# First attention of a two-layer block on one core: each score product replaced by three products of rounded parts

## The chip, the core and the metric

The kernel runs on one core of a Trainium2 chip. The core has a matmul engine (TensorE, PE in the profile; PEld is its weight load), three engines for elementwise work (VectorE or DVE, ScalarE or ACT, GpSimd or POOL), DMA queues and two on-chip memories, SBUF (128 partitions) and PSUM, into which TensorE writes. The metric is the time on the device of the whole program, in microseconds (us); three runs of the kernel before gave 3018.31, 3018.81 and 3020.53 us.

## What is computed

The program runs two blocks one after the other on 512 tokens of width 1024. The change touches one stage of the first block alone, the differential attention of its first layer:

```python
def diff_attn_core(q, k, v, lam):
    s = jnp.einsum('bqhcd,bkhcd->bhcqk', q.astype(jnp.float32), k.astype(jnp.float32))
    p = jax.nn.softmax(s * (1.0 / math.sqrt(HEAD_DIM)), axis=-1)
    a = p[:, :, 0] - lam * p[:, :, 1]
    return jnp.einsum('bhqk,bkhe->bqhe', a.astype(v.dtype), v)
```

There are 8 heads. A head has two components (c = 0, 1) of 64 dimensions, each with its own softmax, and values of 128 dimensions. The queries are 512 tokens, the keys 768 (256 context tokens and the 512 tokens). Before it come the projections to Q, K and V with a norm per head and a rotation; after it a norm per head, the product with `w_o` and the residual.

## The kernel before

Every large product of the program is made of three: a float32 operand x is split into a high part, x rounded to the type F32R, and a low part, x minus the high part, and high by high, high by low and low by high are added in PSUM. The high part is a ScalarE copy, the low part a subtraction on VectorE or GpSimd. The score product of this attention is an exception: it multiplies float32 Q by float32 K at once.

`first_mixer` writes the stage in two blocks. The first makes the projections: Q and K in transposed form (a head's two components on partitions 0 to 63 and 64 to 127), then the rotation by VectorE with one multiplication by GpSimd (L1480), and V in 24 pieces whose evacuation is ScalarE's (L1460). At its end ScalarE loads the table for Exp and computes the lambda (L1469).

The second block is the attention. Its work is cut into 32 units, four (128 queries each) for each head. A unit u passes through these steps:

- `scores(u)` (PE, L1618): for 512 and then 256 keys, component 0 and component 1, one product each into `sc`, four PSUM banks that all units share. It waits for both maxima of unit u - 1 (`top`).
- `negated(u)` (DVE, L1781, twice, one for each component): reads the scores from PSUM, writes them negated into `pr` and takes their extreme. When both are done, `sc` is free for the next unit.
- Exp with its sum (ACT, L1729, twice).
- the weights of the difference: a reciprocal (L1791), a 128x1 product (L1793), and `weighed(u)`, a 128x768 multiply-add of the two components (L1798), all DVE.
- `turn(u)` (PE, L1628, six transposes) and their copy to SBUF (`evacuate`, ACT, L1709).
- `values_product` (PE, L1637): the product with V of the whole previous head, in three parts behind the turns of units 0, 1 and 2 of a head. Behind unit 3's stand instead the sums of squares (L1645), and on DVE the copy of a head's output (L1759).

PE's order is written out: scores of u + 2, turn of u, then the part of the values. DVE's is `negated(u + 1)`, the three weight steps of u. ACT's is the copy of the turn of u - 2, the two Exps of u. Semaphores say when a step may start: `top` (L1781 to L1618), `scores` (L1618 to L1781), `exp`, `differences` (L1798 to L1628), `turned_copied`. GpSimd has nothing to do in this block.

Of the kernel before, what the change touches and what calls it, by code (L numbers as in the profile page):

```python
# [8 lines left out]
F32 = mybir.dt.float32  # L9
F32R = mybir.dt.float32r  # L10
# [5 lines left out]
P = 128  # L16
D = 1024
KD = D // P
NX = 512
# [69 lines left out]
def build(nc, io, ctx):  # L89
# [1097 lines left out]
    def first_mixer(nxt):  # L1187
# [24 lines left out]
        for name, at in homes.items():  # L1212
# [4 lines left out]
                  nc.alloc_sbuf_tensor_at("value_w_high1", [P, KD, 2 * P], F32R, offset=homes["A"])[:]]  # L1217
        v_low = [nc.alloc_sbuf_tensor_at("value_w_low0", [P, KD, NT], F32R, offset=xy_at)[:, :, NX:NT],
                 nc.alloc_sbuf_tensor_at("value_w_low1", [P, KD, 2 * P], F32R, offset=homes["B"])[:]]
        pr = [placed(f"first_prob{b}", (120 + 6 * b) * K1, [P, 2, NT]) for b in range(2)]  # L1220
        weighed = [placed(f"first_weighed{b}", (24 + 4 * b) * K1, [P, NT]) for b in range(2)]
        aT = [placed(f"first_turned{b}", (72 + 12 * b) * K1, [P, KT, NX]) for b in range(2)]
# [10 lines left out]
        sums = slice(HD // 4 - 2, HD // 4)  # L1233
        UNITS = 4 * KT
        BK = {4 + 2 * hd: hd for hd in range(HEADS)}

        def window(hd):

# [27 lines left out]
        if True:  # L1266
# [113 lines left out]
            @block.scalar  # L1380
            def _(scalar):
                follows(scalar, prior)
                def w_high(i):
                    s = i // 2 % 2
                    scalar.wait_ge(ring.landed[s], 16 * (n0[s] + i // 4 + 1))
                    if last_use(i) is not None:
                        scalar.wait_ge(fm["product"].sem, last_use(i) + 1)
                    scalar.activation(split[home_of[i]][0], ring.buf[:, s, i % 2 * T1:(i % 2 + 1) * T1], ACT.Copy)\
                        .then_inc(fm["w_high"].sem, 1)

                def evacuate(i):
                    scalar.wait_ge(fm["product"].sem, i + 1)
                    if i >= 2:
                        scalar.wait_ge(fm["head_summed"].sem, i - 1)
                    if i < HEADS:
                        scalar.activation(Q[:, i, :], ps[:, i % 4, :], ACT.Copy)
                        scalar.activation(sq[:, i % 2, 0:NX], ps[:, i % 4, :], ACT.Square).then_inc(fm["evacuated"].sem, 1)
                        return
                    t = i - HEADS
                    for c, (a, n) in enumerate(STREAMS):  # L1400
                        scalar.activation(K[:, t, a:a + n], ps[:, 2 * (t % 2) + c, 0:n], ACT.Copy)
                        mm = scalar.activation(sq[:, i % 2, a:a + n], ps[:, 2 * (t % 2) + c, 0:n], ACT.Square)
                    mm.then_inc(fm["evacuated"].sem, 1)

                def v_split(v):
                    scalar.wait_ge(ring.landed[v % 2], 16 * (n0[v % 2] + 4 + v // 2 + 1))
                    if v < 2:
                        scalar.wait_ge(fm["product"].sem, 15 + v)
                    else:
                        scalar.wait_ge(fm["v_product"].sem, KT * (v - 1))  # L1410
                    scalar.activation(v_high[v % 2], ring.buf[:, v % 2, :].rearrange("p (k n) -> p k n", k=KD), ACT.Copy)\
                        .then_inc(fm["v_high"].sem, 1)

                w_high(0)
                token_roots(scalar, NT)
                for i in range(1, 3):
                    w_high(i)

                def in_high(k, c):
                    a, n = STREAMS[c]  # L1420
                    scalar.wait_ge(fm["scaled"].sem, c * KD + k + 1)
                    scalar.activation(h_high[:, k, a:a + n], full[:, k, a:a + n], ACT.Identity,
                                      bias=shift[:, k, c:c + 1]).then_inc(fm["in_high"].sem, 1)

                for k in range(KD):
                    in_high(k, 0)
                    if k in (0, 2, 4):
                        w_high(3 + k // 2)
                scalar.wait_ge(fm["tables_ready"].sem, 1)
                evacuate(0)  # L1430
                evacuate(1)
                for k in range(KD):
                    in_high(k, 1)
                w_high(6)
                w_high(7)
                for i in range(2, 5):
                    evacuate(i)
                w_high(8)
                for i in range(5, 7):
                    evacuate(i)  # L1440
                w_high(9)
                evacuate(7)
                w_high(10)
                evacuate(8)
                scalar.wait_ge(fm["head_summed"].sem, HEADS)
                scalar.activation(rows_q[0:HB], ps[0:HB, 6, :], ACT.Sqrt, bias=eps[0:HB, 0:1], scale=1.0 / HD)\
                    .then_inc(fm["rows_rooted"].sem, 1)
                w_high(11)
                for i in range(9, 13):
                    evacuate(i)  # L1450
                    w_high(i + 3)
                evacuate(13)
                evacuate(14)
                v_split(0)
                evacuate(15)
                v_split(1)
                for z in range(UNITS):
                    scalar.wait_ge(fm["v_product"].sem, z + 1)
                    v, m = z // KT, z % KT
                    scalar.activation(V[:, m, v * 2 * P:(v + 1) * 2 * P], ps[:, z % 4, 0:2 * P], ACT.Copy)\  # L1460
                        .then_inc(fm["v_evacuated"].sem, 1)
                    if z == 0:
                        scalar.wait_ge(fm["head_summed"].sem, 2 * HEADS)
                        for c, (a, n) in enumerate(STREAMS):
                            scalar.activation(rows_k[0:HB, a:a + n], ps[0:HB, 4 + c, 0:n], ACT.Sqrt, bias=eps[0:HB, 0:1],
                                              scale=1.0 / HD).then_inc(fm["rows_rooted"].sem, 1)
                    if z in (KT - 1, 2 * KT - 1):
                        v_split(2 + z // KT)
                scalar.activation(lamt[:, 2:4], lamt[:, 0:2], ACT.Exp).then_inc(fm["lambda_exp"].sem, 1)  # L1469

            @block.gpsimd
            def _(gpsimd):
                follows(gpsimd, prior)
                for i in range(3):
                    w_low(gpsimd, i)
                for i in range(2 * HEADS):
                    hd, which = i % HEADS, i // HEADS
                    T = (Q, K)[which]
                    gpsimd.wait_ge(fm["head_swapped"].sem, i + 1)
                    gpsimd.tensor_tensor(T[:, hd, 0:NX], T[:, hd, 0:NX], rope[:, which, :], ALU.mult)\  # L1480
                        .then_inc(fm["head_cos"].sem, 1)

            @block.vector
            def _(vector):
# [113 lines left out]
        if True:  # L1598
# [10 lines left out]
            def _(pe):  # L1609
                follows(pe, prior)  # L1610
                def scores(u):
                    hd, q = u // QT, u % QT
                    if u > 0:
                        pe.wait_ge(fm["top"].sem, 2 * u)
                    for a, n in STREAMS:
                        for c in range(2):
                            rows = slice(c * HD, (c + 1) * HD)
                            mm = pe.matmul(sc[:, c, a:a + n], Q[rows, hd, q * P:(q + 1) * P], K[rows, hd, a:a + n],  # L1618
                                           start=True, stop=True)
                            if a > 0:  # L1620
                                mm.then_inc(fm["scores"].sem, 1)

                def turn(u):
                    pe.wait_ge(fm["differences"].sem, u + 1)
# [77 lines left out]
            def _(scalar):  # L1702
# [21 lines left out]
                for u in range(tiles):  # L1724
                    if u >= 2:
                        evacuate(u - 2)
                    for c in range(2):
                        scalar.wait_ge(fm["top"].sem, 2 * u + c + 1)
                        scalar.activation(pr[u % 2][:, c, :], pr[u % 2][:, c, :], ACT.Exp, bias=top[:, u % 2, c:c + 1], scale=-1.0,  # L1729
                                          accum_out=total[:, c, u:u + 1]).then_inc(fm["exp"].sem, 1)  # L1730
                    if u >= 2 * QT and u % QT == 0:
                        square(u // QT - 2)
                    if u == 1:
                        wo_split(0)
                evacuate(tiles - 2)
# [12 lines left out]
                for m in range(KD):  # L1748
                    if m == KD - 1:
                        scalar.activation(warm[:, 0:1], eps[:], ACT.Sqrt)  # L1750
                    scalar.wait_ge(fm["wo_added"].sem, m + 1)
                    square_tile(scalar, m, xy[:, m, 0:NX], NX)

            @block.vector
            def _(vector):
# [1824 lines left out]
```

## Time and profile before

| | us |
|---|---|
| median of three runs | 3018.81 |
| lowest, highest | 3018.31, 3020.53 |
| the profiled execution | 3019.73 |
| its span in the profile | 3017.9 |
| first score product to last L1781 of the stage | 826.75 to 957.2 |

A row of a timeline gives start and duration in us, engine, line, operation, tiles and shape, and in brackets how long the engine had been idle and who ended that. The durations of matmuls are modelled and overlap: the distance from one start to the next is what a matmul occupies.
### The profile page before, as it was taken

The numbers are of one execution on the slowest core, as the hardware profiler recorded it, in microseconds if no ns is written. First come the engines' busy times: TensorE is split into PE (matmuls) and PEld (weight loads), VectorE is DVE, ScalarE is ACT, GpSimd is POOL, SyncE is SP. The second block draws the span as 40 slices with busy tenths as digits, with TensorE's granted clock in tenths as the row PEclk, the third lists the DMA queues.
The fourth block names the chain that finished last, engine by engine and source line by source line (L and its number), as shares of the span: only waits on it lengthen the run. The fifth ranks groups of instructions, "written<-read, shape, count | busy, mean of one in ns | idle before, by whom it ended". The sixth has DMA issues, their size and how long they took to land.

```text
span 3017.9 us, 37895 instructions
## 1 busy us (share of the span) xinstructions
PE 2908.4 (96%) x15078; PEld 2266.5 (75%) x15078; DVE 1379.6 (46%) x2216; ACT 903.3 (30%) x1441; POOL 287.2 (10%) x318
## 2 busy tenths in 40 slices
PE   8999999999989999999999999999999988999995
PEld 7888888877845888788888888888888855864442
DVE  5646343545577565564333365333332277521113
ACT  4111112232166322223222244222233265321111
POOL 1000000001100100001000031000010164012221
PEclk9999999999989999999999999999999999999998
DMA  7232323221000365453223232232232200448885
GB/s 287 102 132 98 133 103 127 88 76 56 29 1 1 119 247 213 174 209 108 97 84 104 79 131 70 90 104 98 84 115 97 91 29 1 186 170 354 362 353 231
DMA packets 78350, 395.02 MB, mean 131 GB/s; under 512 B 17552, under 2 KB 19984, under 8 KB 51472
## 3 DMA queue, kind: packets, MB, share of 16 engines
q1 hardware_dynamic: 66704, 384.87, 34.7%
q0 software_dynamic: 11520, 8.43, 0.9%
q8 instruction: 85, 1.39, 0.2%
q14 instruction: 41, 0.34, 0.0%
HBM read 443.56 MB, written 16.78 MB: 153 GB/s over the span
## 4 chain that ended last, share of the span: by engine, by line
PE 90%; DVE 6%; ACT 2%; issue 1%; DMA 1%; POOL 1%; SPq 0%; DVEq 0%; ACTq 0%; POOLq 0%
PE ps L906 17%; PE ps L907 17%; PE ps L908 17%; PE ps L3227 6%; PE ps L3249 3%; PE ps L2261 2%; PE ps L2263 2%; PE ps L2262 2%; PE ps L1618 2%; PE ps L1637 1%; PE ps L1296 1%; PE ps L1297 1%; PE ps L1298 1%; PE ps L3023 1%; PE ps L3025 1%
## 5 line engine op out<-in xcount | busy, mean ns | idle before, releaser
L906 PE MATMUL ps<-h_high_ffn,weights_high_ffn 128*128 128x512 f32 (+1 forms) x1696 | 623.5, 368 | 4.5 <-DVE weights_low_ffn L1067 4.5
L907 PE MATMUL ps<-h_low_ffn,weights_high_ffn 128*128 128x512 f32 (+1 forms) x1696 | 623.5, 368 | 0.0
L908 PE MATMUL ps<-h_high_ffn,weights_low_ffn 128*128 128x512 f32 (+1 forms) x1696 | 623.2, 367 | 0.0
L906 PEld LDWEIGHTS ps<-h_high_ffn,weights_high_ffn 128*128 128x128 f32 x1696 | 320.3, 189 | 57.9 <-issue 4.9
L908 PEld LDWEIGHTS ps<-h_high_ffn,weights_low_ffn 128*128 128x128 f32 x1696 | 320.0, 189 | 53.0
L907 PEld LDWEIGHTS ps<-h_low_ffn,weights_high_ffn 128*128 128x128 f32 x1696 | 320.3, 189 | 52.5
L1008 ACT ACTIVATE weights_high_ffn<-weights 128x2048 fp32r<-128x2048 f32 (+4 forms) x160 | 243.9, 1524 | 330.2 <-PE ps L908 263.6
L1067 DVE TENSOR_TENSOR weights_low_ffn<-weights,weights_high_ffn 128x2048 fp32r<-128x2048 f32 (+4 forms) x160 | 291.7, 1823 | 81.7 <-ACT weights_high_ffn L1008 81.1
L906 PE MATMUL ps<-hidden_high_ffn,weights_high_ffn 128*128 128x512 f32 (+1 forms) x836 | 309.5, 370 | 1.1 <-DVE weights_low_ffn L1067 1.1
L907 PE MATMUL ps<-hidden_low_ffn,weights_high_ffn 128*128 128x512 f32 (+1 forms) x836 | 309.2, 370 | 0.0
L908 PE MATMUL ps<-hidden_high_ffn,weights_low_ffn 128*128 128x512 f32 (+1 forms) x836 | 308.9, 370 | 0.0
L1080 DVE TENSOR_TENSOR tmp<-ps,tmp 128x512 f32<-128x512 f32 x110 | 68.2, 637 | 450.8 <-ACT tmp L1018 450.8
L1018 ACT ACTIVATE tmp<-ps 128x512 f32<-128x512 f32 x110 | 58.7, 554 | 671.0 <-PE ps L908 665.4
L1094 DVE SCALAR_TENSOR_TENSOR xy<-ps,mods,xy 128x512 f32<-128x512 f32 (+1 forms) x112 | 72.4, 671 | 242.0 <-PE ps L908 241.7
L906 PEld LDWEIGHTS ps<-hidden_high_ffn,weights_high_ffn 128*128 128x128 f32 x836 | 157.6, 188 | 28.8 <-DVE weights_low_ffn L1067 1.3
L908 PEld LDWEIGHTS ps<-hidden_high_ffn,weights_low_ffn 128*128 128x128 f32 x836 | 157.5, 188 | 26.9
L907 PEld LDWEIGHTS ps<-hidden_low_ffn,weights_high_ffn 128*128 128x128 f32 x836 | 157.6, 188 | 26.7
L3227 PE MATMUL ps<-big,work 128*64 128x512 f32 x768 | 169.7, 593 | 4.2 <-issue 3.3
L406 DVE CUSTOM_DVE_ANT_0 scratch_ffn<-scratch_ffn 128x1024 f32<-128x1024 f32 x127 | 150.3, 1220 | 1.6 <-DMA scratch_ffn<-in_w_mod 1.6
L3227 PEld LDWEIGHTS ps<-big,work 128*64 128x64 f32 x768 | 65.5, 137 | 104.2 <-issue 104.1
L349 POOL TENSOR_TENSOR weights_low_ffn<-weights,weights_high_ffn 128x512 fp32r<-128x512 f32 x32 | 42.3, 1338 | 654.9 <-ACT weights_high_ffn L340 654.9
L1084 DVE TENSOR_TENSOR hidden_low_ffn<-tmp,hidden_high_ffn 128x512 f32 (+3 forms) x88 | 66.8, 759 | 79.2 <-ACT hidden_high_ffn L1020 79.2
(488 smaller groups left out, 4487.3 us busy)
## 6 DMA issues: line engine op xcount, KB each, us to landing
weights<-in_ffn_gu SPq DMA_DIRECT2D x88, 1024.0 KB, 4.9
big<-in_w_exp_gu SPq DMA_DIRECT2D x32, 2048.0 KB, 13.6
scratch_ffn<-in_w_mod SPq DMA_DIRECT2D x35, 1536.0 KB, 6.5
weights<-in_ffn_d SPq DMA_DIRECT2D x24, 768.0 KB, 4.2
weights<-in_w_in SPq DMA_DIRECT2D x16, 1024.0 KB, 4.9
weights<-in_ffn_d SPq DMA_DIRECT2D x24, 640.0 KB, 3.9
weights<-in_w_exp_dn SPq DMA_DIRECT2D x15, 1024.0 KB, 18.5
hbuf<-in_w_exp_dn SPq DMA_DIRECT2D x12, 1024.0 KB, 19.6
```

The lines of the kernel that those rows point to most:

```text
L406: vector.tensor_tensor_reduce(mod_w[b][:, j, :] if last else mod_product, mod_w[b][:, j, :], cond_row[:, c, :], 1.0, 0.0, ALU.mult, ALU.ad ...
L906: pe.matmul(out, wh, xh, start=(k == 0), stop=False)
L907: pe.matmul(out, wh, xl, start=False, stop=False)
L908: mm = pe.matmul(out, wl, xh, start=False, stop=(k == n - 1))
L1008: scalar.activation(w_high[:, s, 0:n], ring.buf[:, s, 0:n], ACT.Copy).then_inc(high_done[s].sem, 1)
L1067: vector.tensor_tensor(w_low[:, s, 0:n], ring.buf[:, s, 0:n], w_high[:, s, 0:n].bitcast(F32), ALU.subtract).then_inc(ring.used[s], 1)
L1080: vector.tensor_tensor(tmp[:, s, a:a + n], gate_up(s, 1, c), tmp[:, s, a:a + n], ALU.mult)\
L1084: vector.tensor_tensor(a_low[:, at, :].rearrange("p a n -> p (a n)"), tmp[:, s, 0:cols], a_high[:, at, :].rearrange("p a n -> p (a n)").bi ...
L1094: vector.scalar_tensor_tensor(x, down(s, c), g, x, ALU.mult, ALU.add)\
L1618: mm = pe.matmul(sc[:, c, a:a + n], Q[rows, hd, q * P:(q + 1) * P], K[rows, hd, a:a + n], start=True, stop=True)
L3227: mm = pe.matmul(ps[b * CAP:(b + 1) * CAP, 2 + n % 2, :], gT[:, k, b * CAP:(b + 1) * CAP], w[:, k, :], start=(k == 0), stop=(k == KD - 1))
L3249: mm = pe.matmul(y_ps[b * CAP:(b + 1) * CAP, a * HF:(a + 1) * HF], act[n % 2][:, f, b * CAP:(b + 1) * CAP], w[:, f, a * HF:(a + 1) * HF], ...
```

## The change

The scores become three products of rounded parts. `head_high(hd)` (ScalarE) copies head hd of Q and of K into rounded high parts, with room for two heads each; `head_low(hd)` (GpSimd) subtracts them from Q and K and writes the low parts over Q and K themselves. Head 0's are made at the end of the first block: ScalarE's two copies after the last piece of V and ahead of the Exp table's load, GpSimd's two subtractions after them. Those of head h + 1 stand on ScalarE behind the Exps of the second unit of head h. PE waits for a head's low parts ahead of its first unit. Each unit's four products become twelve.

```diff
@@ -1217,6 +1217,9 @@
+        Q_low, K_low = placed("Q_low", 32 * K1, [P, HEADS, NX], F32R), placed("K_low", 48 * K1, [P, HEADS, NT], F32R)
+        Q_high = [v_low[0][:, 2 * b:2 * b + 2, :] for b in range(2)]
+        K_high = nc.alloc_sbuf_tensor_at("K_high", [P, 2, NT], F32R, offset=ring_at + 2 * SLOT * 4)[:]
@@ -1233,6 +1236,20 @@
+        def head_high(scalar, hd):
+
+            scalar.activation(Q_high[hd % 2], Q[:, hd, :].rearrange("p (a n) -> p a n", a=2), ACT.Copy)
+            scalar.activation(K_high[:, hd % 2, :], K[:, hd, :], ACT.Copy).then_inc(fm["in_high"].sem, 1)
+
+        def head_low(gpsimd, hd):
+
+            gpsimd.wait_ge(fm["in_high"].sem, 2 * KD + hd + 1)
+            halves = [T[:, hd, :].rearrange("p (a n) -> p a n", a=2) for T in (Q_low, Q)]
+            gpsimd.tensor_tensor(halves[0], halves[1], Q_high[hd % 2].bitcast(F32), ALU.subtract)\
+                .then_inc(fm["in_low"].sem, 1)
+            gpsimd.tensor_tensor(K_low[:, hd, :], K[:, hd, :], K_high[:, hd % 2, :].bitcast(F32), ALU.subtract)\
+                .then_inc(fm["in_low"].sem, 1)
@@ -1466,6 +1483,8 @@
+                scalar.wait_ge(fm["head_ready"].sem, 2 * HEADS)
+                head_high(scalar, 0)
                 scalar.activation(lamt[:, 2:4], lamt[:, 0:2], ACT.Exp).then_inc(fm["lambda_exp"].sem, 1)
@@ -1479,6 +1498,7 @@
+                head_low(gpsimd, 0)
@@ -1612,13 +1632,18 @@
                     if u > 0:
                         pe.wait_ge(fm["top"].sem, 2 * u)
+                    if q == 0:
+                        pe.wait_ge(fm["in_low"].sem, 2 * KD + 2 * hd + 2)
+                    at, b = slice(q * P, (q + 1) * P), hd % 2
                     for a, n in STREAMS:
-                        for c in range(2):
-                            rows = slice(c * HD, (c + 1) * HD)
-                            mm = pe.matmul(sc[:, c, a:a + n], Q[rows, hd, q * P:(q + 1) * P], K[rows, hd, a:a + n],
-                                           start=True, stop=True)
-                            if a > 0:
-                                mm.then_inc(fm["scores"].sem, 1)
+                        for part in range(3):
+                            for c in range(2):
+                                rows = slice(c * HD, (c + 1) * HD)
+                                left = Q_low[rows, hd, at] if part == 2 else Q_high[b][rows, q // 2, q % 2 * P:(q % 2 + 1) * P]
+                                right = K_low[rows, hd, a:a + n] if part == 1 else K_high[rows, b, a:a + n]
+                                mm = pe.matmul(sc[:, c, a:a + n], left, right, start=(part == 0), stop=(part == 2))
+                                if a > 0 and part == 2:
+                                    mm.then_inc(fm["scores"].sem, 1)
@@ -1730,6 +1755,10 @@
+                    if u % QT == 1 and u // QT + 1 < HEADS:
+                        if u > QT:
+                            scalar.wait_ge(fm["scores"].sem, 2 * (u - 1))
+                        head_high(scalar, u // QT + 1)
                     if u == 1:
                         wo_split(0)
@@ -1750,6 +1779,11 @@
+            @block.gpsimd
+            def _(gpsimd):
+                for hd in range(1, HEADS):
+                    head_low(gpsimd, hd)
```

On PE, at a unit whose scores open a head, the row of instructions is first this (before; two operands at once, four products), and then, in the kernel after, twelve. `value_w_low` is the buffer in which Q's high part lies now.

```order
L1618 MATMUL ps<-K,Q 128x512 [waits first_top]
L1618 MATMUL ps<-K,Q 128x512
L1618 MATMUL ps<-K,Q 128x256 x2
L1628 MATMUL ps<-ident,first_weighed_4289 128x128 [waits first_turned_copied,first_differences]
L1628 MATMUL ps<-ident,first_weighed_4289 128x128 x5
```

The same place after:

```order
L1644 MATMUL ps<-K_high,value_w_low_4285 128x512 [waits first_in_low,first_top]
L1644 MATMUL ps<-K_high,value_w_low_4285 128x512
L1644 MATMUL ps<-K_low,value_w_low_4285 128x512 x2
L1644 MATMUL ps<-K_high,Q_low 128x512 x2
L1644 MATMUL ps<-K_high,value_w_low_4285 128x256 x2
L1644 MATMUL ps<-K_low,value_w_low_4285 128x256 x2
L1644 MATMUL ps<-K_high,Q_low 128x256 x2
L1653 MATMUL ps<-ident,first_weighed_4292 128x128 [waits first_turned_copied,first_differences]
```

The turn stands behind twelve products and, once a head, behind a wait for GpSimd (`in_low`).

On ScalarE, the end of the first block and the first units of the attention, before:

```order
L1469 ACTIVATE lamt<-lamt 128x2
L1701 UNCONDITIONAL_BRANCH
L1729 ACTIVATE first_prob_4287,total<-first_prob_4287,top 128x768 [waits first_top,first_head_ready,first_v_evacuated]
L1729 ACTIVATE first_prob_4287,total<-first_prob_4287,top 128x768 [waits first_top]
L1729 ACTIVATE first_prob_4288,total<-first_prob_4288,top 128x768 [waits first_top] x2
L1722 ACTIVATE out_w_high_4297<-weights 128x2048 [waits slab_landed0]
```

and after:

```order
L1242 ACTIVATE value_w_low_4285<-Q 128x2x256 [waits first_head_ready]
L1243 ACTIVATE K_high<-K 128x768
L1488 ACT_TABLE_LOAD
L1488 ACTIVATE lamt<-lamt 128x2
L1726 UNCONDITIONAL_BRANCH
L1754 ACTIVATE first_prob_4290,total<-first_prob_4290,top 128x768 [waits first_top,first_head_ready,first_v_evacuated]
L1754 ACTIVATE first_prob_4290,total<-first_prob_4290,top 128x768 [waits first_top]
L1754 ACTIVATE first_prob_4291,total<-first_prob_4291,top 128x768 [waits first_top] x2
L1242 ACTIVATE value_w_low_4285<-Q 128x2x256
L1243 ACTIVATE K_high<-K 128x768
L1747 ACTIVATE out_w_high_4300<-weights 128x2048 [waits slab_landed0]
```

Two copies stand ahead of the table load, and two behind the Exps of the second unit of every head but the last. GpSimd's queue gets sixteen subtractions, in pairs (Q's 128x512, then K's 128x768), between its last rotation and its first work of the next stage.

## Rows read from the trace of the kernel before

**Rows 1.** The page: engines of the chain that ended last.

```profile
PE 90%; DVE 6%; ACT 2%; issue 1%; DMA 1%; POOL 1%; SPq 0%; DVEq 0%; ACTq 0%; POOLq 0%
```

**Rows 2.** Windows of the attention: busy time and instructions by engine, PEclk, DMA share, GB/s.

```profile
831.24:844.90 13.66, 11.28 (x36) 5.53 (x35) 7.62 (x17) 7.34 (x13) 0.00 (x0) 0.50 0.00 0
858.55:956.00 97.45, 94.64 (x470) 50.43 (x469) 82.34 (x182) 69.86 (x131) 0.00 (x0) 1.00 0.00 1
```

**Rows 3.** Timeline, PE, one unit with a values part: turn, values, next scores.

```profile
889.17 0.88 PE L1628 MATMUL ps<-ident,first_weighed 128*128 128x128 f32 x6
889.88 1.88 PE L1637 MATMUL ps<-first_turned,V 128*128 128x512 f32 x4
891.69 1.56 PE L1618 MATMUL ps<-K,Q 64*128 64x512 f32 x8
893.18 0.33 PE L1628 MATMUL ps<-ident,first_weighed 128*128 128x128 f32 x1
```

**Rows 4.** Timeline, DVE, three cycles of head 3, first rows of each.

```profile
885.77 0.96 DVE L1781 CUSTOM_DVE_ANT_0 first_prob<-ps,column 128x768 f32<-128x768 f32 x1 [0.19 <-PE ps L1618]
889.27 0.96 DVE L1781 CUSTOM_DVE_ANT_0 first_prob<-ps,column 128x768 f32<-128x768 f32 x1 [0.26 <-PE ps L1618]
891.22 0.22 DVE L1793 SCALAR_TENSOR_TENSOR total<-total,lamt 128x1 f32<-128x1 f32 x1
891.48 1.02 DVE L1798 SCALAR_TENSOR_TENSOR first_weighed<-first_prob,total 128x768 f32<-128x768 f32 x1
893.28 0.96 DVE L1781 CUSTOM_DVE_ANT_0 first_prob<-ps,column 128x768 f32<-128x768 f32 x1 [0.79 <-PE ps L1618]
```

**Rows 5.** Timeline, ACT, a copy of 768 in F32R, then the second Exp of a unit.

```profile
58.31 0.85 ACT L1020 ACTIVATE hidden_high_ffn<-tmp 128x768 fp32r<-128x768 f32 x1 [0.88 <-DVE tmp L1080]
888.21 0.93 ACT L1729 ACTIVATE first_prob<-first_prob,top 128x768 f32<-128x768 f32 x1
```

**Rows 6.** Timeline, PE, F32R products at full clock, 256 and 512 columns.

```profile
809.73 0.28 PE L1370 MATMUL ps<-value_w_high,first_h_high 128*128 128x256 f32 x1
809.85 0.28 PE L1371 MATMUL ps<-value_w_low,first_h_high 128*128 128x256 f32 x1
986.19 0.39 PE L1680 MATMUL ps<-out_high,out_w_low 128*128 128x512 f32 x1
986.42 0.39 PE L1678 MATMUL ps<-out_high,out_w_high 128*128 128x512 f32 x1
```

**Rows 7.** Timeline, PE, one unit's scores at half clock.

```profile
840.63 2.93 PE L1618 MATMUL ps<-K,Q 64*128 64x512 f32 x8 [0.46 <-DVE top L1781]
```

**Rows 8.** Timeline, the passage between the two blocks: ACT and DVE.

```profile
826.71 1.28 ACT L1469 ACT_TABLE_LOAD   x1
829.15 0.96 DVE L1781 CUSTOM_DVE_ANT_0 first_prob<-ps,column 128x768 f32<-128x768 f32 x1
```

**Rows 9.** Groups by shape, POOL: subtractions of 512 and of 1024.

```profile
L349 POOL TENSOR_TENSOR weights_low_ffn<-weights,weights_high_ffn 128x512 fp32r<-128x512 f32 x32 | 42.3, 1338 | 654.9 <-ACT weights_high_ffn L340 654.9
L1258 POOL TENSOR_TENSOR head_w_low_R<-weights,head_w_high_R 128x1024 fp32r<-128x1024 f32 x1 | 2.4, 2359 | 541.9 <-ACT head_w_high_R L1388 541.9
```

**Rows 10.** Timeline, POOL and DVE side by side in the rotation.

```profile
812.35 1.30 POOL L1480 TENSOR_TENSOR K<-K,rope_tables 128x512 f32<-128x512 f32 x1 [6.08 <-DVEq L1535]
812.36 1.83 DVE L1536 TENSOR_TENSOR tmp<-tmp,sine_tables 128x512 f32<-128x512 f32 x1
814.23 0.69 DVE L1539 TENSOR_TENSOR tmp<-tmp,K 128x512 f32<-128x512 f32 x1
```

**Rows 11.** Timeline, second block's attention: small DVE steps under POOL's in a row.

```profile
2444.88 0.83 POOL L2628 TENSOR_TENSOR work<-work,stat 128x384 f32<-128x384 f32 x1
2444.97 0.76 DVE L2658 TENSOR_SCALAR stat<-stat 128x8 f32<-128x8 f32 x1
2445.66 0.83 POOL L2628 TENSOR_TENSOR work<-work,stat 128x384 f32<-128x384 f32 x1
2445.76 0.74 DVE L2659 TENSOR_TENSOR stat<-stat,sinks 128x2 f32<-128x2 f32 x1
```

## The prediction

> **What bounds the kernel now.** I read the chain that ended last first: TensorE carries 90% of it [rows 1], so a gain or loss on PE's path counts in full, and nothing outside the attention stage is touched. Then the windows of the stage: half clock from 831.24 to 844.90 while it starts, full clock from 858.55 on [rows 2]. Then the timelines of its steady part. A cycle, from the first L1781 of one unit to that of the next, is 3.50 us once a head and 4.01 us three times [rows 4], 15.5 us a head.
>
> In a 4.01 cycle PE is the bound: turn 0.71 (889.17 to 889.88), values 1.81, scores 1.49 (891.69 to 893.18) [rows 3], while DVE waits 0.79 us for the scores [rows 4]. In the 3.50 cycle, which has no values, the loop through `sc` binds: DVE needs 1.95 from the first L1781 to L1793, 0.26 to L1798, 1.02 for it, 3.23 in all, and then waits 0.26 for scores [rows 4].
>
> **The scores.** One unit's four float32 products take 1.49 us and are replaced by twelve F32R ones. If the two components' products run side by side, each pair costs what one product costs. A 512-column F32R product occupies 0.23 us (986.19 to 986.42), a 256-column one 0.12 [rows 6]. Three pairs of each are 1.05. I add 0.20 for the first load and the change to 128 rows: that is what 1.49 holds over two times 512 and 256 columns at 2.4 GHz, two cycles a column (1.28), which is also what shows that the components now run side by side (one after the other would be 2.56). New scores: 1.25, so 0.24 saved. Bounds: 1.18, if a pair costs its bare columns, and 2.3 if the two rounded products of a pair run in turn, as no row shows F32R on 64 partitions. I take the near end, as the row groups already run together in this very line. At half clock the scores take 2.93 [rows 7]; F32R would take three times 768 columns at 1.2 GHz, 1.92, plus 0.3: 2.2, so 0.65 saved.
>
> The Trainium skill, "TensorE: Matmul & The Clock Gate", Part 3, The mechanism, says that products in different row groups of the array overlap with starts some 4 ns apart. It gives no exception for this type. By it the scores are the 1.25 above; no run here shows it for F32R yet.
>
> Undisturbed, a 4.01 cycle would become 3.77 and the 3.50 one 3.24 (DVE's 3.23 is then the floor). With 0.1 for the output copy that DVE has to fit in, a head is 14.65 to 14.7: 0.85 saved.
>
> **The first head's parts.** ScalarE is free at 826.71 [rows 8]. Q's copy (512) is some 0.55, K's 0.85 [rows 5], Q's scaled from it. GpSimd starts at 828.2; its subtractions are 1.3 for 512 and, between 1.34 and 2.36 [rows 9], 1.84 for 768: done at 831.3. Now nothing covers this: PE has finished V, DVE waits. PE's first scores start at 831.4, by then at half clock (the clock is low from 831.24 on [rows 2], when PE had idled since its first scores, for some 2.7 us until L1781 freed `sc`; here it has idled for five), and take 2.2. The first L1781 moves from 829.15 [rows 8] to 833.7: **+4.5**. At full clock it is 1 less. The table load behind the copies ends at 829.5, hidden.
>
> **Units 0 to 7.** A cycle at half clock is 1.95 - 0.05 to free `sc`, 2.93 for the scores, 4.86 with the release; it becomes 4.2. Three such cycles fill the half-clock stretch [rows 2]: **-1.6**. From unit 3 to 8 I count +0.2: the further savings go against the conflict below, which head 1 has as well, and a return to half clock.
>
> **The later heads: GpSimd beside VectorE.** In the attention GpSimd is idle now; the change gives it 3.1 us a head. What that does to DVE is in the rotation: L1536, a product of two SBUF inputs, started with a GpSimd product and took 1.83 instead of 0.69 [rows 10]. It ended 0.55 after GpSimd's, its own data time. So it stood still until GpSimd was done. Even steps of a few columns do: 0.74 to 0.76 us under GpSimd's 0.83, and the next such step was caught by GpSimd's next instruction in turn [rows 11]. L1793 and L1798 have two SBUF inputs each; L1781 reads PSUM and isn't of that kind.
>
> The Trainium skill, "SBUF — State Buffer", Who interferes with whom, speaks against the change in the same sense: a VectorE instruction with two SBUF inputs and a GpSimd one that reads SBUF share an exclusive lock, held for the whole instruction by whichever came first. By this rule alone up to both subtractions a head fall on DVE. The trace agrees (1.83 for 0.69).
>
> Where they meet, from t = 0 at the first L1781 of a head's second unit, with cycles of 3.24 and 3.77: the second Exp starts at 2.44 (888.21 less 885.77) and ScalarE is free 0.93 later [rows 4, 5]. Copies until 4.75, GpSimd's Q subtraction 4.83 to 6.14, K's to 7.94. DVE's next L1781 starts at 3.24, its L1793 would at 5.2: 0.4 too late, it stands until 6.16. GpSimd's next instruction then comes first, and L1798 stands until 7.94 and needs 0.82 more (768 columns at the rate of the 0.55): 8.76 instead of 6.50. PE has wanted it for the turn since 3.24 + 3.77 = 7.0. So 1.8 us are lost, and L1781 behind it is as late. A head becomes 14.65 + 1.8 = 16.45, 0.9 more than now. PE's own wait for the low parts is covered: it wants them with the scores of the fourth cycle. ScalarE's 1.4 us a head lie in its idle time beside the values.
>
> Heads 2 to 6 carry this, five times 0.9: **+4.6**. Head 7 makes no parts for a next one: **-0.5** for the cycles that still end in the stage.
>
> **Sum:** 4.5 - 1.6 + 0.2 + 4.6 - 0.5 = +7.2. On the profiled execution (3019.73) that is 3026.9; it lay 0.9 over the median, so the forecast for the median is 3018.8 + 7.2 = **3026.0**. The stage's end has no DMA to wait for and what follows is PE's, so nothing gives this back.
>
> **Rivals.**
>
> 1. *Only one subtraction is caught (not slower).* Same mechanism, decided by 0.4 us: if ScalarE's copies end 0.4 later or L1793 starts 0.4 earlier, L1793 gets by, L1798 stands until the Q subtraction alone is done (6.5 + 0.8 = 7.4 against 7.0), and a head is 15.1 or, later still, 14.7. That is -0.5 to -0.85 for five heads, against +0.9: the sum falls to between 0 and -2, **3017 to 3019**. For it: the margin is small against copies whose strided output of 2x256 no row shows. Against it: all pieces but that are rows of steady cycles. 18%.
> 2. *The pairs run in turn.* Scores 2.3: 0.8 more than now in 27 or so cycles, with the start: **3048**. Only a missing row speaks for it. 7%.
> 3. *The clock falls again.* PE idles 1.8 us in a head where it was busy [rows 2]. If half clock came back for a stretch of a few us in each of five heads, each would cost 2 to 3.5 us: **3036 to 3043**. Against it: some 2.7 us of idling, after a start with little work, went before the fall at 831.24, and here PE is full between the gaps. 8%.
> 4. *A real gain.* No conflict counts and the start costs only 3.5 (full clock at the first scores, and the half-clock stretch shorter by half, 2.5 us more): 3.5 - 2.5 - 1 - 6 x 0.9 = -5.4, with 1.18 for the scores -7, **3012 to 3013.5**. 6%.
>
> The forecast's case has the remaining 61%; its own range, from 1.18 for the scores, 0.3 either way in where the parts meet, and the start between 3.4 and 5, is 3022 to 3030.
>
> **Range and chances.** 3016.5 to 3036: it takes in rival 1 but its lowest edge, and the forecast's case with a mild third rival; outside lie the second, most of the third and the fourth. The least that a measurement of this kernel can tell is about 0.2%, 6 us: the bounds are 3012.8 and 3024.8. The forecast's case puts two thirds over 3024.8, rivals 2 and 3 all: slower 0.56. Rival 1, a third of the forecast's case and a third of rival 4: same 0.40. The rest, faster, 0.04.
>
> **What would show it.** Twelve score products with starts of pairs under 0.01 us apart, the scores taking 1.25: else rival 2. The first L1781 at about 833.7. In each of heads 1 to 6 one L1793 of 0.8 to 1 us instead of 0.22 and one L1798 of about 2.5 instead of 1.02, in the cycle after the head's second unit, and a cycle of 5.4 there with three under 4.0. If only L1798 is long, rival 1. PEclk under 1.00 between 860 and 960: rival 3. I am wrong altogether if L1798 keeps 1.02 while GpSimd works beside it, or if PE waits for `in_low` at the start of later heads.

## The result and the profile after

| | median us | runs | ratio to before [95% interval] |
|---|---|---|---|
| before | 3017.88 | 20 | |
| after | 3024.20 | 20 | 1.0018 [1.0011, 1.0026] |

The changed kernel is slower by 6.3 us between the medians. The ratio of the table, 1.0018, is not the quotient of the two medians, which is 1.0021. The forecast was +7.2. The interval excludes no change, and it lies on both sides of the 0.2% that the prediction took as its bound, so it does not decide between its two main outcomes, slower and the same. The profiled execution of after has a span of 3023.2 us.

First the groups of after between 815 and 1000 us, by line: busy time, mean ns of one, and the idle time before them with what ended it. L1815 is the old L1781, L1827 the old L1793, L1832 the old L1798, L1653 the turn.

```profile
L1832 DVE SCALAR_TENSOR_TENSOR first_weighed<-first_prob,total 128x768 f32<-128x768 f32 x32 | 41.8, 1307 | 1.1
...
L1653 PE MATMUL ps<-ident,first_weighed 128*128 128x128 f32 x192 | 30.4, 298 | 11.7 <-DVE first_weighed L1832 11.3
...
L1251 POOL TENSOR_TENSOR K_low<-K,K_high 128x768 fp32r<-128x768 f32 x8 | 14.6, 1829 | 0.0
...
L1249 POOL TENSOR_TENSOR Q_low<-Q,value_w_low 128x512 fp32r<-128x512 f32 x8 | 10.2, 1274 | 108.1 <-ACT K_high L1243 108.1
```

L1832 has 32 instructions as before, of the same shape, and takes 41.8 us in all, where 32 times the 1.02 us of before [rows 4] are 32.6. PE waits 11.3 us for it ahead of the turn. Where the 9.2 us lie is seen in DVE's timeline of head 3, from the first L1815 of its second unit on:

```profile
890.20 0.96 DVE L1815 CUSTOM_DVE_ANT_0 first_prob<-ps,column 128x768 f32<-128x768 f32 x1
...
893.60 0.96 DVE L1815 CUSTOM_DVE_ANT_0 first_prob<-ps,column 128x768 f32<-128x768 f32 x1 [0.17 <-PE ps L1644]
...
895.37 0.16 DVE L1825 RECIPROCAL total<-total 128x1 f32<-128x1 f32 x1
895.56 0.72 DVE L1827 SCALAR_TENSOR_TENSOR total<-total,lamt 128x1 f32<-128x1 f32 x1
896.31 2.56 DVE L1832 SCALAR_TENSOR_TENSOR first_weighed<-first_prob,total 128x768 f32<-128x768 f32 x1
899.04 0.96 DVE L1815 CUSTOM_DVE_ANT_0 first_prob<-ps,column 128x768 f32<-128x768 f32 x1 [0.17 <-DVE first_weighed L1832]
...
902.79 0.96 DVE L1815 CUSTOM_DVE_ANT_0 first_prob<-ps,column 128x768 f32<-128x768 f32 x1 [0.52 <-PE ps L1644]
```

The same microseconds on GpSimd:

```profile
894.98 1.27 POOL L1249 TENSOR_TENSOR Q_low<-Q,value_w_low 128x512 fp32r<-128x512 f32 x1 [13.29 <-ACT K_high L1243]
896.21 1.85 POOL L1251 TENSOR_TENSOR K_low<-K,K_high 128x768 fp32r<-128x768 f32 x1
```

Read the two together. L1827 works on 128x1 and takes 0.22 us elsewhere. Here it starts 0.58 into Q's subtraction and ends 0.03 after it. L1832 comes next, but K's subtraction has begun by then, and L1832 ends 0.81 after that one. The cycle is 899.04 - 893.60 = 5.44 us; the ones around it are 3.40 and 3.75. On PE, in the long cycle, six rows of scores, two products each, and the turn that has waited:

```profile
896.01 0.50 PE L1644 MATMUL ps<-K_high,value_w_low 64*128 64x512 f32 x2
896.35 0.39 PE L1644 MATMUL ps<-K_low,value_w_low 64*128 64x512 f32 x2
896.58 0.40 PE L1644 MATMUL ps<-K_high,Q_low 64*128 64x512 f32 x2
896.81 0.28 PE L1644 MATMUL ps<-K_high,value_w_low 64*128 64x256 f32 x2
896.93 0.27 PE L1644 MATMUL ps<-K_low,value_w_low 64*128 64x256 f32 x2
897.04 0.28 PE L1644 MATMUL ps<-K_high,Q_low 64*128 64x256 f32 x2
898.92 0.88 PE L1653 MATMUL ps<-ident,first_weighed 128*128 128x128 f32 x6 [1.60 <-DVE first_weighed L1832]
```

A row holds two products. From row to row it is 0.23 us for 512 columns and 0.12 for 256, what one F32R product of that width took on 128 rows [rows 6]; only behind the first row it is 0.34. In the trace's times in ns the starts of a pair lie 3 to 4 ns apart. The twelve products end at 897.32 (897.04 + 0.28), and then PE stands 1.60 us.

The start of the stage, on ACT, POOL, PE and DVE:

```profile
827.15 0.38 ACT L1477 ACTIVATE V<-ps 128x256 f32<-128x256 f32 x1 [2.49 <-PE ps L1389]
...
827.43 0.62 ACT L1242 ACTIVATE value_w_low<-Q 128x512 fp32r<-128x512 f32 x1
...
827.95 0.83 ACT L1243 ACTIVATE K_high<-K 128x768 fp32r<-128x768 f32 x1
...
828.86 1.26 POOL L1249 TENSOR_TENSOR Q_low<-Q,value_w_low 128x512 fp32r<-128x512 f32 x1 [14.38 <-ACT K_high L1243]
...
830.08 1.80 POOL L1251 TENSOR_TENSOR K_low<-K,K_high 128x768 fp32r<-128x768 f32 x1
...
832.03 0.79 PE L1644 MATMUL ps<-K_high,value_w_low 64*128 64x512 f32 x2 [4.91 <-POOL K_low L1251]
...
834.43 0.96 DVE L1815 CUSTOM_DVE_ANT_0 first_prob<-ps,column 128x768 f32<-128x768 f32 x1 [1.82 <-PE ps L1644]
```

The first L1815 starts 6.90 us after V's last evacuation has ended (834.43 - 827.53). Before, L1781 started 2.46 after it. PE's 4.91 of waiting for GpSimd occurs this one time in the stage.

Last, the windows of the stage: busy us and instructions of PE, PEld, DVE, ACT and POOL, then PEclk.

```profile
834.00:847.00 13.00, 7.42 (x46) 5.47 (x43) 9.05 (x18) 9.28 (x15) 3.08 (x2) 0.63 0.00 0
847.00:860.70 13.70, 11.05 (x54) 8.56 (x54) 11.66 (x23) 7.88 (x16) 0.00 (x0) 0.50 0.00 1
860.70:959.00 98.30, 85.58 (x549) 55.31 (x547) 91.12 (x174) 74.21 (x140) 18.39 (x12) 1.00 0.00 1
```

From 860.7 to 959 the granted clock is 1.00 throughout, with PE idle for 12.7 us of it. Ahead of that there was more half clock than before the change: 830.0 to 843.7 and 847.1 to 860.7, 27.3 us in all, where before it was 20.5 (831.2 to 844.9 and 851.7 to 858.6).

Measured over both traces by the starts of L1781 and of L1815, the stage from V's last evacuation to the last of its 32 units grew by 6.5 us (128.75 to 135.25), in three pieces:

| piece | before | after | difference | forecast |
|---|---|---|---|---|
| V's end to the first L1815 | 2.46 | 6.90 | +4.4 | +4.5 |
| first L1815 to that of unit 8 | 37.07 | 35.62 | -1.45 | -1.4 |
| unit 8 to unit 31 | 89.21 | 92.73 | +3.5 | +4.1 |

### The profile page after: what moved, and what is told of

Read it like the earlier page. It is cut to its first block, busy times and chain, and to the rows that moved or that the text cites. A ratio compares the mean times of both kernels' runs of the same rounds, so it can differ in the third digit from the quotient of the medians.

```text
span 3023.2 us, 38190 instructions
## 1 busy us (share of the span) xinstructions
PE 2902.5 (96%) x15206; PEld 2279.9 (75%) x15206; DVE 1394.4 (46%) x2216; ACT 911.9 (30%) x1457; POOL 311.1 (10%) x334
## 4 chain that ended last, share of the span: by engine, by line
PE 88%; DVE 7%; ACT 2%; issue 1%; DMA 1%; POOL 1%; SPq 0%; DVEq 0%; ACTq 0%; POOLq 0%
PE ps L906 17%; PE ps L907 17%; PE ps L908 17%; PE ps L3261 5%; PE ps L3283 3%; PE ps L2295 2%; PE ps L2296 2%; PE ps L2297 2%; PE ps L1313 1%; PE ps L1314 1%; PE ps L1315 1%; PE ps L3057 1%; PE ps L1662 1%; PE ps L3059 1%; PE ps L3058 1%
## 5 line engine op out<-in xcount | busy, mean ns | idle before, releaser
L2295 PE MATMUL ps<-mixer_h_high,mixer_w_high 128*128 128x512 f32 x256 | 100.1, 391 | 1.6 <-DVE mixer_h_low L2445 1.3
```

The costliest lines, as they stand in the source:

```text
L2295: pe.matmul(out, w_high[:, s, at], h_high[:, k, :], start=(k == 0), stop=False)
```

## The experiments

The theory on trial: both of a head's subtractions on GpSimd stop VectorE, one instruction after the other; this turns a gain of 0.85 us a head into a loss, and apart from it the price of the change lies in the uncovered start. The medians and ratios of each run are against the kernel before on the same chip (3019.18 us for the first four, 3017.48 for the rest). "A head" is the time from the first L1815 of a head's second unit to that of the next head's, in the profiled execution: 15.53 us before.

**The changed kernel again (after_again)**, unedited, to see which of its numbers repeat.

> The changed kernel once more, as the measure for the runs beside it. All theories: 5 to 8 us over the kernel before; first L1815 at about 834.4; a head from 860 on 16.4 us, of which one cycle 5.4; L1832 2.55 us once in each of heads 2 to 6.

3024.67 us, ratio 1.0019 [1.0008, 1.0030]. A head from the third on is 16.34 to 16.37 in both traces, the long cycle 5.42 to 5.44, the first L1815 comes 6.78 after V's end (6.90). What does not repeat is the piece from the first L1815 to unit 8: 34.73 against 35.62, with 27.3 us of half clock in both, but in other stretches. So numbers of that piece are good to about 1 us.

**K's subtraction waits for one VectorE step (k_waits).** Nothing is left out; GpSimd starts the second subtraction only when the L1832 that it would have met has finished.

```diff
+            if hd > 0:
+                gpsimd.wait_ge(fm["differences"].sem, 4 * (hd - 1) + 2)
             gpsimd.tensor_tensor(K_low[:, hd, :], K[:, hd, :], K_high[:, hd % 2, :].bitcast(F32), ALU.subtract)\
```

> One edit: for heads 1 to 7 GpSimd begins K's subtraction only when L1832 of the preceding head's second unit is done (it waits for differences). Both subtractions still run. Theory A (the loss is the second subtraction taking its turn between L1827 and L1832): L1827 keeps its 0.7, L1832 is 1.02 everywhere, the cycle of 5.4 becomes 3.8, a head 14.7 instead of 16.4, which over six heads is 9 to 10 us under the changed kernel and about 3 us under the kernel before; K's subtraction ends at some 9.1 us after the head's second L1815, PE wants it at 9.6. Theory B (GpSimd at work slows VectorE in general, whatever it has started): L1832 or other VectorE steps stay long, no gain. Theory C (the 5.4 comes from ScalarE's two copies, which put off the Exps): no gain.

3013.47 us, ratio 0.9985 [0.9974, 0.9996]: 11.2 below the changed kernel beside it. A head is 14.82. GpSimd's timeline in head 3 (in this run L1832 of after is L1834, L1827 is L1829 and L1815 is L1817; each of the runs below has its own shift):

```profile
890.73 1.27 POOL L1249 TENSOR_TENSOR Q_low<-Q,value_w_low 128x512 fp32r<-128x512 f32 x1 [10.57 <-ACT K_high L1243]
893.15 1.82 POOL L1253 TENSOR_TENSOR K_low<-K,K_high 128x768 fp32r<-128x768 f32 x1 [1.15 <-DVE first_weighed L1834]
```

and DVE's:

```profile
892.06 1.02 DVE L1834 SCALAR_TENSOR_TENSOR first_weighed<-first_prob,total 128x768 f32<-128x768 f32 x1
893.25 0.96 DVE L1817 CUSTOM_DVE_ANT_0 first_prob<-ps,column 128x768 f32<-128x768 f32 x1 [0.17 <-ACT first_prob L1756]
...
895.20 0.22 DVE L1829 SCALAR_TENSOR_TENSOR total<-total,lamt 128x1 f32<-128x1 f32 x1
895.46 1.02 DVE L1834 SCALAR_TENSOR_TENSOR first_weighed<-first_prob,total 128x768 f32<-128x768 f32 x1
```

K's subtraction takes the same 1.82 us, but now it lies beside L1817, which reads PSUM and keeps its 0.96, and is over (894.97) before L1829 comes at 895.20. The work is the same; only its place has changed, and 1.54 us a head are back. The long L1832 and its price are thus shown to come from K's subtraction lying where it lay. ScalarE's two copies stay where they were, so they are not what made the long cycle. L1829 still stands under Q's subtraction, 0.72 us, and that costs 0.13: the cycle is 3.90, where it is 3.77 without. One long L1834 is left against the expectation, 1.93 us in head 1, where it meets Q's subtraction. Of the 11.2 us, 7.7 lie between unit 8 and unit 31 (84.99 against 92.73); 3.1 lie in units 0 to 7 (32.56 against 35.62), where this profile had 17.1 us of half clock and after 27.3.

**No subtractions from head 1 on (no_low).** The products read the high parts in place of the low ones there.

```diff
             halves = [T[:, hd, :].rearrange("p (a n) -> p a n", a=2) for T in (Q_low, Q)]
+            if hd > 0:
+                gpsimd.sem_inc(fm["in_low"].sem, 1)
+                gpsimd.sem_inc(fm["in_low"].sem, 1)
+                return
...
```

> GpSimd's subtractions for heads 1 to 7 are left out, and the products that would read their low parts read the high parts instead; ScalarE's copies and all twelve products stay. Theory A: as k_waits, and L1827 0.22 everywhere: a head 14.65 to 14.7, 9.5 to 10.5 us under the changed kernel. If this is under k_waits by over 1 us, the first subtraction costs something too. Theory C: a head stays over 16.

3015.54 us, ratio 0.9987 [0.9974, 1.0000]. The groups of the stage:

```profile
L1836 DVE SCALAR_TENSOR_TENSOR first_weighed<-first_prob,total 128x768 f32<-128x768 f32 x32 | 32.6, 1019 | 1.1
...
L1831 DVE SCALAR_TENSOR_TENSOR total<-total,lamt 128x1 f32<-128x1 f32 x32 | 7.0, 219 | 1.1
```

Both steps are back at their means of before, and a head is 14.70, in cycles of 3.40, 3.77, 3.76 and 3.77. This is the undisturbed head of the forecast (14.65 to 14.7). The median is 2.1 us over that of k_waits, which does more; the two intervals overlap over nearly their whole width, so the two times are not told apart, and the heads of the profiles are. The whole conflict is thus worth 16.36 - 14.70 = 1.66 us a head, and with only the small step held 0.12 of it is left (k_waits).

**The old scores with all the preparation (old_scores).** Four float32 products read the two tiles of the low parts, taken as plain float32; copies, subtractions and waits stay.

```diff
...
-                                mm = pe.matmul(sc[:, c, a:a + n], left, right, start=(part == 0), stop=(part == 2))
...
+                            mm = pe.matmul(sc[:, c, a:a + n], Q_low[rows, hd, at].bitcast(F32), K_low[rows, hd, a:a + n].bitcast(F32),
+                                           start=True, stop=True)
...
```

> The scores are four float32 products again (of the low parts, which now lie where Q and K did, so the scores' values are others); all copies and subtractions stay. It prices the preparation without the cheaper scores. Theory A: L1832 stays caught, its end hangs on GpSimd and not on the scores, so in the long cycle little changes, and the three others are 0.24 longer: a head about 16.9, and with the half-clock cycles 0.65 longer each some 5 to 7 us over the changed kernel, 11 to 13 over the kernel before. If F32R pairs bought nothing, it would equal the changed kernel.

3028.58 us, ratio 1.0038 [1.0025, 1.0051]. A head is 16.83, with cycles of 3.49, 5.33, 4.00 and 4.02. The conflict alone therefore costs 16.83 - 15.53 = 1.30 us a head, and with it present the new scores return 0.47 of the 0.83 that they return in its absence (15.53 - 14.70). The long cycle gets nothing from them: 5.33 with the old, 5.44 with the new. That is as it must be, since in it PE waits for DVE. In the whole it was 3.9 over the changed kernel, where 5 to 7 were expected; the piece up to unit 8 had only 6.8 us of half clock in this profile, and took 33.5 us.

**The first head's copies earlier (early).** They stand ahead of the last three of V's evacuations, so that both engines prepare head 0 while PE still computes V.

```diff
-                scalar.wait_ge(fm["head_ready"].sem, 2 * HEADS)
-                head_high(scalar, 0)
+                    if z == 3 * KT + 2:
+                        scalar.wait_ge(fm["head_ready"].sem, HEADS + 1)
+                        head_high(scalar, 0)
```

> One part of the changed kernel moved: head 0's two copies stand on ScalarE behind the evacuation of V's piece 20 of 0 to 23, as soon as head 0 of K is rotated; GpSimd's two subtractions follow at once, while PE still makes V. If the start costs what the sum says (nothing covers the parts of head 0), the first L1815 comes 2.5 us after V's last evacuation instead of 6.8 to 6.9, the rest stays, and the kernel is 4.4 us under the changed one: 1 to 3 us over the kernel before. If half clock makes the start dear instead, and sets in anyway, less than 3 of them come back.

3018.52 us, ratio 1.0002 [0.9994, 1.0011]: no difference from before.

```profile
819.92 1.84 POOL L1251 TENSOR_TENSOR K_low<-K,K_high 128x768 fp32r<-128x768 f32 x1
...
826.02 0.50 PE L1645 MATMUL ps<-K_high,value_w_low 64*128 64x512 f32 x2 [0.47 <-ACT V L1477]
...
828.43 0.96 DVE L1816 CUSTOM_DVE_ANT_0 first_prob<-ps,column 128x768 f32<-128x768 f32 x1
```

K's low part is there at 821.76, nearly four microseconds before PE is done with V. PE waits 0.47 us for V's evacuation instead of 4.91 for GpSimd, and the first L1816 comes 2.47 after V's end, as before (2.46). In the profiles the start's 4.4 us are thus all recovered. Its heads are still 16.36.

**The two subtractions in the other order (k_first).** K's 128x768 first, Q's 128x512 behind it.

> The two subtractions of a head change places: K's (1.83) first, then Q's (1.27). If VectorE and GpSimd take turns, one instruction each, the first catches L1827 and the second L1832 whatever their sizes: L1827 1.25 instead of 0.72, L1832 about 2.0 instead of 2.55, both ending where they did, and a head stays 16.36 us. If L1832 hung on K's subtraction by itself, it would be short and a head under 16.

3024.03 us in a single run; its heads, and not its time, are the measurement. POOL and DVE in head 3, in order of time:

```profile
893.48 1.83 POOL L1249 TENSOR_TENSOR K_low<-K,K_high 128x768 fp32r<-128x768 f32 x1 [13.31 <-ACT K_high L1243]
...
894.05 1.28 DVE L1827 SCALAR_TENSOR_TENSOR total<-total,lamt 128x1 f32<-128x1 f32 x1
...
895.26 1.27 POOL L1251 TENSOR_TENSOR Q_low<-Q,value_w_low 128x512 fp32r<-128x512 f32 x1
...
895.36 1.99 DVE L1832 SCALAR_TENSOR_TENSOR first_weighed<-first_prob,total 128x768 f32<-128x768 f32 x1
```

The small step is now held by the longer subtraction and lasts 1.28 instead of 0.72; the large one is held by the shorter, 1.99 instead of 2.56. Each lost what the other gained, and the head stayed at 16.36. Whichever instruction comes second on GpSimd here, the step of DVE that stands behind the first gets through only between the two, and the next one meets the second. Between these two orders the sizes decide nothing but the split.

**Both repairs together (between_early)**, with the later heads' copies a unit earlier as well and each subtraction behind the end of an L1832 of the preceding head (the first unit's for Q, the second unit's for K).

```diff
+            if hd > 0:
+                gpsimd.wait_ge(fm["differences"].sem, 4 * (hd - 1) + 1)
             gpsimd.tensor_tensor(halves[0], halves[1], Q_high[hd % 2].bitcast(F32), ALU.subtract)\
                 .then_inc(fm["in_low"].sem, 1)
+            if hd > 0:
+                gpsimd.wait_ge(fm["differences"].sem, 4 * (hd - 1) + 2)
... (and the edit of early)
-                    if u % QT == 1 and u // QT + 1 < HEADS:
-                        if u > QT:
-                            scalar.wait_ge(fm["scores"].sem, 2 * (u - 1))
+                    if u % QT == 0 and u // QT + 1 < HEADS:
+                        if u > 0:
+                            scalar.wait_ge(fm["scores"].sem, 2 * u)
```

> early, and the copies of the next head one unit sooner (behind the Exps of a head's first unit), each subtraction started by the end of one L1832 (first unit's: Q, second unit's: K). All the rounded work stays. With both costs gone: L1827 0.22 and L1832 1.02 everywhere, a head 14.7, first L1815 2.5 us behind V: the stage, from V's end to the last L1815, 120 us instead of 134 to 135 (before: 129), the kernel 9 us under the one before (0.997). If ScalarE's copies at their new place put off the Exps of the second unit, a head is up to 15.3, and 4 us of this are missing.

3008.40 us, ratio 0.9966 [0.9954, 0.9978]. POOL and DVE around the two subtractions of head 3:

```profile
885.51 1.27 POOL L1251 TENSOR_TENSOR Q_low<-Q,value_w_low 128x512 fp32r<-128x512 f32 x1 [9.53 <-DVE first_weighed L1837]
885.54 0.96 DVE L1820 CUSTOM_DVE_ANT_0 first_prob<-ps,column 128x768 f32<-128x768 f32 x1 [0.17 <-PE ps L1649]
...
887.50 0.22 DVE L1832 SCALAR_TENSOR_TENSOR total<-total,lamt 128x1 f32<-128x1 f32 x1
...
887.75 1.02 DVE L1837 SCALAR_TENSOR_TENSOR first_weighed<-first_prob,total 128x768 f32<-128x768 f32 x1
...
888.85 1.83 POOL L1255 TENSOR_TENSOR K_low<-K,K_high 128x768 fp32r<-128x768 f32 x1 [2.06 <-DVE first_weighed L1837]
...
889.30 0.96 DVE L1820 CUSTOM_DVE_ANT_0 first_prob<-ps,column 128x768 f32<-128x768 f32 x1 [0.53 <-PE ps L1649]
```

Q's subtraction is over at 886.78, before the weight steps at 887.50; K's starts 0.08 after L1837's end. Both lie beside steps that read PSUM. All 32 weight products take 0.22 us and all 32 of the large ones 1.02; a head is 14.70, as if GpSimd did nothing, and the start is 2.46. The kernel is 9.1 us under before, where 9 were expected.

**And the table load earlier (best)**: lambda's Exp, which brings ScalarE's table load with it, moves behind head 0's copies too.

> between_early, and the Exp of lambda with its table load moved ahead too, behind head 0's copies. Then only the first scores stand between V and the first L1815: 1.6 us instead of 2.5, and 0.8 to 1 us less in all; if PE's clock falls less for it, up to 3.

3007.88 us, ratio 0.9968 [0.9957, 0.9980]. The first score step comes 1.53 after V's end instead of 2.46, so the load had held the start once the subtractions no longer did. In the whole that isn't seen: 0.5 us between two medians whose intervals overlap, and the piece up to unit 8 took 34.54 in this profile against 33.65. Whether the 0.9 us are kept or given back there is open.

## Why the forecast was right, and where it was not

**The conflict (+0.9 a head).** It took place as worked out, at the steps that were named, in each of heads 2 to 6: measured +0.83. From t = 0 at the first L1815 of the second unit (890.20):

| | forecast | measured |
|---|---|---|
| second Exp starts | 2.44 | 2.44 |
| Q's subtraction starts | 4.83 | 4.78 |
| L1827 begins, and ends | 5.2, 6.16 | 5.36, 6.08 |
| K's subtraction ends | 7.94 | 7.86 |
| PE wants the turn | 7.0 | 7.12 |
| L1832 ends | 8.76 | 8.67 |

L1827 took 0.72 us where 0.8 to 1 was forecast, since it came 0.16 later and was free 0.08 earlier. In head 1 L1832 is as long (2.56), and L1827 took 0.63.

The Trainium skill, "SBUF — State Buffer", Who interferes with whom, calls the lock one for the whole instruction and says "Issue order, not op shape, decides who blocks." k_first agrees with this (1.28 and 1.99 us, head unchanged), and so does L1815, which with one SBUF input keeps 0.96 beside a subtraction (k_waits). What the row of a 128x1 step costs beside it, 0.72 or 1.28 us for 0.22, the run shows by itself.

**The scores (1.25).** From 901.45, where they start in the next cycle, to the turn at 902.69 it is 1.24. At half clock: forecast 2.2, measured 2.29 (832.03 to 834.32). The starts of a pair lie 3 to 4 ns apart, so rival 2 is out, and rows on 128 partitions turned out to be good for 64. The Trainium skill, "TensorE: Matmul & The Clock Gate", Part 3, The mechanism, has such products overlap with starts about 4 ns apart; at full clock the trace agrees for this type.

**The short cycle (3.24): this term was mis-sized.** It is 3.40. The forecast took DVE's own work, 3.23, as the floor. But L1815 has to wait for the step just ahead of it on the same engine: it overwrites a buffer which that L1832 has read, and the program has it wait for `differences`. The row says so, `[0.17 <-DVE first_weighed L1832]`, and a gap of 0.17 us stands in every cycle in which nothing comes later, under other names too. That the wait makes the gap is argued from the program and the rows; no run left it out. Before, scores came 0.26 late [rows 4] and covered it. The sum of a head hardly shows this (14.70 against 14.65): the 0.1 that I had added for the output copy isn't to be seen (3.75 to 3.78 in the cycles with and without it), so one error stood against the other.

**The start (+4.5)** measured +4.4. The chain was right, link by link: copies, two subtractions, scores at half clock. early shows that it was all due to the place of the copies.

**Units 0 to 7 (-1.4)** measured -1.45 in one trace and -2.3 in the other. With a spread of 1 us between two traces of the same kernel the agreement in the first says little, and part of it is luck. The prediction's sum is wrong here: three cycles that shrink from 4.86 to 4.2 save 1.95 to 2.0, where it wrote 1.6. The first three cycles did save 1.62 (14.44 to 12.82), as the first of before was 4.72 and the third of after 4.37, and the half clock lasted 6.8 us longer than before (27.3 against 20.5), where the prediction counted on one stretch and left its return and head 1's conflict to the +0.2. With 1.95 its whole sum would have been +6.9.

**Unit 8 to 31 (+4.1)** measured +3.5. The five heads gave +4.1 where +4.6 was forecast, and the cycles at the two ends -0.6 where it was -0.5.

**"Nothing gives this back"** holds for the stage's end but cannot be shown for the whole. In the two profiled executions the lag of after is 8.6 us at the first group of L3227 in the second block's last part and 5.4 at its last group. Before:

```profile
2687.71 7.09 PE L3227 MATMUL ps<-big,work 128*64 128x512 f32 x32 [0.89 <-DVE work L3295]
...
2976.62 7.07 PE L3227 MATMUL ps<-big,work 128*64 128x512 f32 x32
```

and after:

```profile
2696.30 7.09 PE L3261 MATMUL ps<-big,work 128*64 128x512 f32 x32 [0.89 <-DVE work L3329]
...
2982.01 7.07 PE L3261 MATMUL ps<-big,work 128*64 128x512 f32 x32
```

In that part the one profile of before is longer by 2.8 to 3.7 us than eight of the nine profiles of changed kernels, early and between_early among them, whose stage is as short as before's or shorter, and by 0.5 than that of old_scores. So it does not follow the length of the stage. Whether it belongs to that one execution of before was not tested. The medians, +6.3, agree with the stage's +6.5.

**The rivals.** Rival 1 needed L1827 to get by. It missed by more than the 0.4 us forecast: the subtraction was 0.58 old. k_waits made a near relative of that rival, with one step held instead of two, but the small one by Q's subtraction and L1832 free; it gave 14.82 a head. Rival 3: PEclk 1.00 in all the stretch from 860.7 to 959, with 1.60 us of idling in each head. Rival 4's real gain needed the absence of both costs, and between_early, which removes both, has it: -9.1, more than the -5.4 to -7 of the rival, which still paid 3.5 for the start.

## What to carry to other kernels

In this kernel work given to an idle GpSimd wasn't free while VectorE had steps with two SBUF inputs. In another with such steps, look on VectorE's timeline for the steps that read PSUM or one SBUF tile and tie each GpSimd instruction to the semaphore of the step ahead of them, one wait for each instruction. (L1825, which reads one, kept its 0.16 us under Q's subtraction.) Here the two subtractions of a head cost 1.66 us unplaced, 0.12 with one wait, and nothing with two and the copies a unit earlier. And what a later unit has covered, the first unit of a stage has not: prepare it in the stage ahead.

## What was not expected of the hardware

Three things, with their numbers.

- Between L1832's end and the next L1815, which waits for it on the same engine, lie 0.17 us in every changed kernel here. It is no price of every such wait: L1827 and L1832 also wait for the step just ahead of them, and start 0.03 to 0.04 us after it (896.28 to 896.31). Those follow a 128x1 step and L1815 a 128x768 one; whether that makes the difference was not tested.
- Once two GpSimd instructions stand in a row, they and VectorE's two-input steps take turns one by one, even where VectorE's next step is ready 0.03 us after its last: both were held, 0.72 and 2.56 us, or 1.28 and 1.99 in the other order. GpSimd itself lost next to nothing: K's subtraction took 1.85 us in head 3, and 1.82 in k_waits, where it met no two-input step.
- A step on one column is held as a large one is. [rows 11] had such small steps at 0.74 to 0.76 us; at the start lambda's 128x1 difference took 1.56 us beside K's subtraction, for 0.16 in early:

```profile
830.34 1.56 DVE L1600 TENSOR_TENSOR lamt<-lamt 128x1 f32<-128x1 f32 x1 [13.85 <-ACT lamt L1488]
```

It was hidden, as PE needed the low parts until later anyway.
